# Weight blocks behind a norm split early in places of their own, and operand low parts made by VectorE alone

## What is computed

```python
h = _layer_norm(ALPHA * h + 0.5 * _swiglu(h, ffn1_w_gate, ffn1_w_up, ffn1_w_down), ln1_g, ln1_b)
mix = _token_mixers(h, w_in, ...)
h = _layer_norm(ALPHA * h + mix, ln2_g, ln2_b)
h = _layer_norm(ALPHA * h + _memory_cross_attention(h, mem, ...), ln3_g, ln3_b)
h = _layer_norm(ALPHA * h + 0.5 * _swiglu(h, ffn2_w_gate, ffn2_w_up, ffn2_w_down), ln4_g, ln4_b)
q, k, v, u = split(rmsnorm(h, norm1_g) @ w_in_2)
x = h + concatenate([attention_mixer(q, k, v), pool_mixer(u)]) @ w_out_2
x = x + (silu(rmsnorm(x, norm2_g) @ w_gate) * (... @ w_up)) @ w_down
```

## Time and profile before

| | before |
|---|---|
| median of 3 runs | 1681.72 us (1681.31 to 1683.2) |
| the profiled execution | 1679.79 us, its span 1677.2 us |
| PE busy | 1653.6 us, 99% of the span |
| DVE, ACT, POOL busy | 655.5, 596.2, 706.9 us |
| granted clock of PE | 1.00 (0.999 over the span) |

### The profile page before, as it was taken

The page is one execution under the profiler, slowest core; times in us unless marked ns, Lnnn a source line. Parts: engine busy times, 40 slices in busy tenths (PEclk is TensorE's granted clock), DMA queues, the critical chain, the costliest instruction groups (busy, mean ns, idle before and its releaser), DMA issues.

```text
span 1677.2 us, 20695 instructions
## 1 busy us (share of the span) xinstructions
PE 1653.6 (99%) x8327; PEld 1387.6 (83%) x8327; DVE 655.5 (39%) x1064; ACT 596.2 (36%) x909; POOL 706.9 (42%) x395
## 2 busy tenths in 40 slices
PE   9999999999999999999999999998999999999998
PEld 7888888898888888898888888897768988888887
DVE  4111111267665776657121211167763612121122
ACT  4222222247445564436221222257573422222220
POOL 4453444445572352116443444354321644344432
PEclk9999999999999999999999999999999999999999
DMA  7333233333222444123333243242111433324322
GB/s 208 91 98 101 77 112 100 88 116 103 70 64 64 126 140 137 51 63 101 101 92 97 82 116 92 88 132 64 45 32 53 112 101 101 89 81 119 95 82 76
DMA packets 296520, 157.57 MB, mean 94 GB/s; under 512 B 5233, under 2 KB 293098, under 8 KB 296426
## 3 DMA queue, kind: packets, MB, share of 16 engines
q1 hardware_dynamic: 296426, 156.26, 32.4%
HBM read 154.14 MB, written 2.10 MB: 93 GB/s over the span
## 4 chain that ended last, share of the span: by engine, by line
PE 90%; DVE 4%; ACT 4%; issue 1%; POOL 0%; DMA 0%; DVEq 0%; SPq 0%; ACTq 0%
PE bank L505 22%; PE bank L506 22%; PE bank L509 22%; PE bank L549 2%; PE bank L548 2%; PE bank L553 2%; PE bank L2788 2%; PE bank L2324 1%; PE bank L2318 1%; PE bank L2319 1%; PE bank L534 1%; PE bank L528 1%; PE bank L529 1%; ACT res L1033 1%; PE bank L2776 1%
## 5 line engine op out<-in xcount | busy, mean ns | idle before, releaser
L435 POOL TENSOR_TENSOR wlo<-wraw,whi 128x1024 fp32r<-128x1024 f32 (+1 forms) x252 | 596.6, 2381 | 826.5 <-ACT whi L430 826.4
L505 PE MATMUL bank<-ahi,whi 128*128 128x512 f32 x1294 | 507.7, 392 | 0.0
L506 PE MATMUL bank<-alo,whi 128*128 128x512 f32 x1294 | 503.8, 389 | 0.0
L430 ACT CAST whi<-wraw 128x1024 fp32r<-128x1024 f32 (+1 forms) x284 | 285.0, 1027 | 236.8 <-PE bank L509 153.5
L509 PE MATMUL bank<-ahi,wlo 128*128 128x512 f32 x1294 | 320.9, 389 | 0.0
L505 PEld LDWEIGHTS bank<-ahi,whi 128*128 128x128 f32 x1294 | 243.0, 188 | 51.3 <-issue 1.2
L506 PEld LDWEIGHTS bank<-alo,whi 128*128 128x128 f32 x1294 | 243.0, 188 | 51.2 <-issue 1.4
L509 PEld LDWEIGHTS bank<-ahi,wlo 128*128 128x128 f32 x1294 | 242.9, 188 | 50.4
L1612 DVE SCALAR_TENSOR_TENSOR hval<-gate,bank 128x512 f32<-128x512 f32 x66 | 45.4, 688 | 546.6 <-PE bank L509 539.4
L993 ACT ACTIVATE gate<-bank 128x512 f32<-128x512 f32 x66 | 39.5, 599 | 501.8 <-PE bank L509 496.6
L1621 DVE SCALAR_TENSOR_TENSOR res<-res,bank 128x512 f32<-128x512 f32 x80 | 54.1, 686 | 251.4 <-PE bank L509 179.0
(11 more groups left out here) (361 smaller groups left out, 2227.6 us busy)
## 6 DMA issues: line engine op xcount, KB each, us to landing
wraw<-in_ffn_w_gate SPq DMA_DIRECT2D x43, 512.0 KB, 3.8
wraw<-in_ffn_w_up SPq DMA_DIRECT2D x43, 512.0 KB, 3.8
wraw<-in_w_in SPq DMA_DIRECT2D x34, 512.0 KB, 3.9
wraw<-in_ffn_w_down SPq DMA_DIRECT2D x32, 512.0 KB, 3.7
wraw<-in_w_gate SPq DMA_DIRECT2D x22, 512.0 KB, 3.8
wraw<-in_w_up SPq DMA_DIRECT2D x22, 512.0 KB, 3.8
wraw<-in_w_out SPq DMA_DIRECT2D x16, 512.0 KB, 4.4
wraw<-in_w_down SPq DMA_DIRECT2D x16, 512.0 KB, 3.6
```

Of the source, the lines that this page charges most:

```text
L430: eng.copy(high_of(b)[:, 0:n], raw_of(b)[:, 0:n]).then_inc(hi_ready, 1)
L435: eng.tensor_tensor(low_of(b)[:, 0:n], raw_of(b)[:, 0:n], high_of(b)[:, 0:n], ALU.subtract).then_inc(LO[b][0], 1)
L505: eng.matmul(o, w, xhi[:, k, :], start=(k == 0), stop=False)
L506: eng.matmul(o, w, xlo[:, k, :], start=False, stop=False)
```

## The change

Four buffers of their own are added in memory that is free around a norm: `early_raw` and `early_lo`, two places in one room, and `early_hi`, four places. Blocks x+2 and x+3 are loaded into `early_raw` as soon as p+0 is done (`load_early`, ahead of p+6 on SP); x+0 and x+1 stay in `wraw`. All four have their high parts in `early_hi`, so their cast waits for no `whi` place. The order of splits around a norm becomes p+4, x+2, p+5, x+3, p+6, p+7, x+0, x+1 (it was p+4 to p+7, then x+0 to x+3), and on ACT all of it now stands ahead of the first half's square of tile 6. POOL makes the low parts of x+0 to x+3 at every norm, and of the p blocks as before (at ln3 and rms2 DVE makes those of p+5 and p+7). All low parts of operand tiles are made by DVE (`HALF_MAKERS = [DVE] * KD`). At ln4 ACT makes all 16 squares of rms1 and POOL adds them up, where POOL made two and DVE added. On PE, the low products of x+1 stand in their natural place (`LATE` is gone), and the means of the second half come one tile earlier (`STATS_AT` 3, was 4).

```diff
+        early_at = arena + WORK + 48 * KB + 4 * SKEW
+        early_raw = sb("early_raw", [P, 2, KD * P], at=early_at)
+        early_lo = sb("early_lo", [P, 2, KD * P], F32R, at=early_at)
+        early_hi = sb("early_hi", [P, 4, KD * P], F32R, at=early_at + 8 * KB)
...
+        for ph, nx in NORM_AT:
+            p, x = ph.base, nx.base
+            SPLITS[p + 5:x + 4] = [x + 2, p + 5, x + 3, p + 6, p + 7, x, x + 1]
+        RAW_RING = [b for b in range(len(blocks)) if b not in EARLY_RAW]
+        HI_RING = [b for b in SPLITS if b not in EARLY_HI]
...
+        def load_early(eng, ph):
+            n = [x for x, _ in NORM_AT].index(ph)
+            nx = NORM_AT[n][1]
+            wait_block(eng, ph, 0)
+            for i in range(2):
+                src = nx.src(1, i) if nx.kind == "up" else nx.src(2 + i)
+                dst = early_raw[:, i, :].rearrange("p (k f) -> p k f", f=nx.width)
+                eng.dma_start(dst, src).then_inc(early_ready[i], 16)
...
-        HALF_MAKERS = [DVE, POOL, DVE, POOL, DVE, POOL, POOL, DVE]
+        HALF_MAKERS = [DVE] * KD
...
-            STATS_AT = 4
+            STATS_AT = 3
...
                 for j in range(4):
                     hi_stream(ph, j)
+                    if j in (1, 2):
+                        split_hi(act, nx.base + j + 1)
                     square_tile(ph, norm, j)
                 hi_stream(ph, 4)
                 for j in range(4, KD):
                     square_tile(ph, norm, j, 0)
+                    if j < 6:
+                        split_hi(act, nx.base + j - 4)
                 square_tile(ph, norm, 4, 1)
...
-            def tail(ph, nx, norm):
-                for j in range(6):
+            def tail(ph, nx):
+                for j in range(5):
                     lo_stream(ph, j)
-                low(norm, 0, 1)
-                lo_stream(ph, 6)
...
+                    if j in (1, 2):
+                        pool_weights(pool, nx.base + j + 1)
+                for j in range(2):
+                    pool_weights(pool, nx.base + j)
```

More of the change, by code:

```diff
@@ L301, in build @@
         hi_ready = sem("hi_ready")
+        early_ready = [sem(f"early_ready{i}") for i in range(2)]
         raw_quarter = [sem(f"raw_quarter{i}") for i in range(3)]
@@ L591, in low_half @@
         def low_half(norm, h, k):
+            if norm == "ln4":
+                return ln4_low, 8 * h + k + 1
             own = HALF_MAKERS[k]
@@ L597, in square_made @@
         def square_made(h, k):
[L599 to L602, removed]
+            return rms1_squares, KD * h + k + 1
         def mean_of(norm):
@@ L921, in stream @@
                 for j in range(4 if ph.base == 0 else 0, ph.n):
+                    if j == 6 and any(ph is x for x, _ in NORM_AT):
+                        load_early(sp, ph)
                     load_block(sp, ph, j)
@@ L1090, in scale_norm_halves @@
             def scale_norm_halves(ph, nx, norm):
-                tail(ph, norm)
+                tail(ph, nx, norm)
                 rstd_half(norm, 0)
-                hi_stream(ph, 5)
                 cast(norm, 0, 0)
@@ new lines, in tail, with one_norm @@
+            def tail(ph, nx):
+                for j in range(5):
+                    lo_stream(ph, j)
+                    if j in (1, 2):
+                        pool_weights(pool, nx.base + j + 1)
+                for j in range(2):
+                    pool_weights(pool, nx.base + j)
+            def one_norm(ph, nx, norm):
+                tail(ph, nx)
+                for h in range(2):
+                    for k in range(KD):
+                        low(norm, h, k)
+            def two_norms_halves(ph, nx):
+                tail(ph, nx)
+                for k in range(1, KD):
+                    add_square(0, k)
+                for k in range(1, KD - 1):
+                    add_square(1, k)
@@ L1520, in _ @@
                 split_lo(pool, b)
-            ffn("f1", lambda ph: tail(ph, phases["in"], "ln1"))
+            ffn("f1", lambda ph: one_norm(ph, phases["in"], "ln1"))
             def level_args(s):
@@ L1564, in _ @@
                     lo_stream(phases[name], j)
-            tail(phases["xo"], phases["f2_up0"], "ln3")
+            one_norm(phases["xo"], phases["f2_up0"], "ln3")
             ffn("f2", lambda ph: two_norms_halves(ph, phases["in2"]))
@@ L1736, in tail @@
                 sum_tile(norm, 4, 1)
-                if norm != "rms2":
-                    lo_stream(ph, 5)
             def layer_norm_halves(ph, nx, norm, alpha):
@@ L1795, in scale_norm_halves @@
                 rescale(norm, 0, 6)
+                low(norm, 0, 5)
                 rescale(norm, 0, 7)
+                low(norm, 0, 6)
                 low(norm, 0, 7)
-                lo_stream(nx, 0)
                 for k in range(KD):
@@ L1828, in two_norms_halves @@
                 add_half(ph, "ln4", 6, 1, alpha)
+                low("ln4", 0, 1)
                 standardise("ln4", 0, 4)
+                standardise("ln4", 0, 5)
                 add_half(ph, "ln4", 7, 1, alpha)
+                sum_tile("ln4", 6, 1)
                 low("ln4", 0, 2)
-                sum_tile("ln4", 6, 1)
-                standardise("ln4", 0, 5)
                 standardise("ln4", 0, 6)
+                low("ln4", 0, 3)
                 standardise("ln4", 0, 7)
-                low("ln4", 0, 4)
-                low("ln4", 0, 7)
+                for k in range(4, KD):
+                    low("ln4", 0, k)
                 variance("ln4", 1)
@@ L2369, in pair_half @@
                     pe.matmul(o1, high_of(b1)[:, w], ahi[:, k, at], start=(k == 0), stop=False)
-                    if k == LATE and h == 0:
-                        pe.wait_ge(*LO[b1])
-                    for m in range(0 if k == LATE else k, k + 1 if k >= LATE else k):
-                        pe.matmul(o1, low_of(b1)[:, m * P:(m + 1) * P], ahi[:, m, at], start=False, stop=False)
+                    pe.matmul(o1, low_of(b1)[:, w], ahi[:, k, at], start=False, stop=False)
                     if k:
```

208 lines of the change are left out of this document (89 added, 119 removed).

## The result

The changed kernel takes 1695.05 us (median of 4 runs, 1693.35 to 1695.64), the kernel before beside it 1682.26 us (4 runs, 1681.31 to 1683.2). The ratio is 1.0074, with a 95% interval of 1.0057 to 1.0092: the change costs 12.8 us. The forecast was 1689.0 us, 7.3 more than before, so the sign is as forecast and the size is not: 1695.05 lies above the forecast's own range, 1685 to 1693, and inside the wide one, 1677 to 1696, in the part that was given to the rival *More*.

The account below looks back on a forecast made before the run. TensorE, busy 99% of the span, was taken as the bound, so only its waits count. Head gains of 9.5 us against tail delays of 6.3, 4.2 and 6.3 gave 1681.7 + 7.3 = 1689.0 us, range 1685 to 1693 (wide 1677 to 1696).

Parts of the forecast that it names:

- the rival *More: GpSimd gets in twice in a row, or p+6 and p+7 also keep TensorE waiting: +7.2, 1696 us; chance 0.10.
- What bounds the kernel: TensorE is busy 99% of the span, 24 us at most to be had; only what makes it wait counts.
- Heads of ln1 and ln3, -2.8 each: Casts and splits of x+0 to x+3 leave these heads, winning back the full 2.8 us lost at each.
- Head of ln4, -3.7: ScalarE loses four casts in this head; of 5.7 us lost, 2 of wait stay, so 3.7 us are gained.
- rms2, -0.2: Head at rms2 has hardly a wait; 0.2 us gained there.
- The walk through the tail: Moved GpSimd splits and VectorE sums take turns, delaying the statistics 6.3 us at ln1, 4.2 ln3, 6.3 ln4, 0 rms2.
- The low parts on VectorE at no cost: In the heads, VectorE takes over eight low parts a norm, about 0.34 us each, 2.7 in all; they fit.
- -9.5 + 6.3 + 4.2 + 6.3 = +7.3: Gains at the four heads, 9.5 us, against tail delays at ln1, ln3 and ln4: 7.3 us slower.
- slip between the splits: Rival: the tail's sums fit between the splits, at most 1.0 us of added splits reaches the last; 1672.2 us, chance 0.13.
- half of it: Rival: about 3 us lost in the tail at each layer norm, -0.5 in sum; 1681 us (1678 to 1685), chance 0.19.

Follow-up runs that it names:

- version 6: Changed kernel, VectorE making all weight-block low parts of tail and head, square of tile 1 ahead of block 2's cast: 1674.62 us, ratio 0.9957; repeated, 1673.77 us.
- experiment 1: Changed kernel with GpSimd making the low parts of x+0 to x+3 only after the first half's running sums: 1689.05 us, ratio 1.0043.
- version 5: Changed kernel with low parts of the next matrix's blocks 0 to 3 on VectorE, blocks 4 to 7 of the running phase still on GpSimd: 1683.38 us, ratio 1.0008.
- Experiment 3: Changed kernel with operand tiles' low parts at ln1, ln3 and rms2 divided between VectorE and GpSimd as in the kernel before: 1694.71 us, ratio 1.0074.
- experiment 2: Changed kernel with unread products on TensorE ahead of the first-half sums' wait, 44 at ln1 and ln4, 18 at ln3: 1690.17 us, ratio 1.0049.
- version 4: Changed kernel with ScalarE's square of tile 1 ahead of the early cast of block 2: 1689.99 us, ratio 1.0050.
- 7: Changed kernel with all weight-block low parts of tail and head on VectorE, block 2's cast still ahead of the square of tile 1: 1674.81 us, ratio 0.9962.
- 8: Kernel before, with low parts of blocks 4 to 7 ahead of the four norms on VectorE, nothing split early: 1681.74 us, ratio 0.9998.

## Why the prediction was right in sign and short in size

**What bounds the kernel: right.** All that the change moved lies in TensorE's waits at the norms and in its clock behind them.

**Heads of ln1 and ln3, -2.8 each: right at ln1, 0.7 too much at ln3.** They gave 2.9 and 2.1. A head of 23.8 us was forecast; it is 23.7 at ln1 and 24.5 at ln3. The 23.8 was itself a slip: 23.1 and two products of 0.43 make 24.0. The 0.8 us between the two heads moves between executions, since the repeat of version 6 shows 23.7 at ln3 and 24.5 at ln1; what makes it stays open.

**Head of ln4, -3.7: mis-sized, 2.9.** With the wait for rstd and 1.3 us for rms1's products taken off, it takes 1172.33 - 2.51 - 1142.21 - 1.3 = 26.3 us; near 26 was forecast. I started from 30.7 us before and get 27.6 by the same sum, a gain of 3.1, of which 0.2 are lost again behind the wait.

**rms2, -0.2: wrong by 0.5.** Its head grew by 0.3 us. The sum forecast for the heads was 9.5, measured 7.6.

**The walk through the tail: right in mechanism and nearly in size.** Forecast 6.3, 4.2, 6.3, 0, in sum 16.8; measured 5.5, 2.6, 5.9, 0, in sum 14.0. The steps hold one by one: the square of tile 1 was put at 343.0 and stands at 343.18; six or seven long sums a norm were 7, 5, 7 and 4; the last sum ends at 368.75 for a forecast of 369.5; TensorE's half microsecond for the low part of p+7 is there at ln4 (0.41 us). ln3 was mis-sized, 2.6 for 4.2: with VectorE's two splits only 5 long sums are left there. Experiments 1, 5 and 6 show the exclusion to be the cause, each from another side.

**The low parts on VectorE at no cost: right.** Experiment 3 finds nothing either way at ln1, ln3 and rms2.

**What was missing: TensorE's clock.** The sum priced a stall at its length. Behind each stall the products ran at the lower clock, 7.4 us at the three norms by the traces, of which experiment 2 took back 6.8 there, and 4.9 net by the medians. The version of experiment 2, which has the stalls and not the lower clock, stands 8.4 us above the kernel before in its own comparison (1690.17 and 1681.77), beside a forecast of +7.3. The step that failed is the line of the sum, "-9.5 + 6.3 + 4.2 + 6.3 = +7.3": it has no term for what a standing TensorE costs after it has started again. The terms that it has were off in ways that nearly cancel, which is luck: the heads gave 1.9 us less than forecast and the stalls cost 2.8 less, so that they make +6.4 beside +7.3, and the 7.4 at the lower clock come on top. The "more" rival had the number, 1696, by a mechanism that did not occur: no sum met a second split in a row, and of its other half, waits for p+6 and p+7, only 0.4 us came.

**Rivals.** The sums did not slip between the splits, and "half of it" did not come: the turns are as strict as in the earlier trace rows.

## What to carry to other kernels

Moving work of GpSimd off the critical path is not free where VectorE adds or subtracts tiles that lie in SBUF: count the pairs that meet, and give the moved work to VectorE itself (1.22 us here, 2.40 on GpSimd) if it has the room. Price a wait of TensorE of some 5 us at half as much again, for what follows it at the lower clock (3.0 and 2.7 us behind 5.24 here), and one of 2 to 3.5 us at anything from nothing to 2.0 us, and check the granted clock of the stretch behind every new wait. A stall that a move causes may just move on: after each edit read what waits next, as the low parts in experiment 1.

## What the runs showed of the hardware

A wait of 5.24 us leaves TensorE at a granted clock of 0.50 for some 5 us more: 21 products start in the 5.4 us from 368.8, where 49 do in version 6. Shorter waits can do it too, and then the clock may fall only after products run again: at ln3 in the changed kernel a wait of 2.41 us was followed by 0.8 us at 1.00 and then 3.4 us at 0.52, and in version 4 one of 3.47 us at ln4 by 0.68 over 5.4 us. But they need not: in version 5 a wait of 2.76 us at ln1 was followed by 0.68 over 5.4 us, a longer one of 3.13 us at ln4 by 1.00 over 5.

The same wait in the same kernel goes both ways. The rms1 wait is 2.5 us in every trace; over the 4.7 us behind it the clock was 1.00 in the kernel before, experiments 2, 7 and 8 and the repeat of 6, and 0.64 to 0.68 in the changed kernel, experiments 1, 3, 4 and 5 and the first run of 6. So for these shorter waits neither the length of the wait nor the program settles it; what does stays open (the two runs of 6 were on two chips). Executions on one chip spread by as much: the ten of version 5 took 1680.18 to 1685.06 us, at a mean granted clock of 0.998 in the fastest and 0.995 in the slowest. A difference of 1.5 us between two profiled spans is thus no effect of an edit before the clock has been read behind every long wait of both.

Products whose result nobody reads, put into the waits at ln1, ln3 and ln4, kept the clock at 1.00 behind all three.
